# Modulation vector taken from TensorE to VectorE and ScalarE, one reciprocal for the delta net's head norms, early gates in two banks

## The reference, cut to what matters

```python
# the modulation: one vector for the tokens (c_2), one for the context (c_ctx_2);
# of silu(c) @ mod_w + mod_b the second block takes a shift, a scale and a gate,
# three vectors of 1024. Nothing of the first block goes into it.
h = rms_norm_2(x, norm_g) * (1 + scale) + shift
...
# the delta net's queries and keys, per head of 64 channels
def l2_normalize(x):
    return x * lax.rsqrt(jnp.sum(x * x, axis=-1, keepdims=True) + EPS)
...
# a branch's gate: a full 1024 x 1024 product of the same h for each branch
gate = jax.nn.sigmoid(h @ w_gate[i] + b_gate[i])
```

## Time and profile before

| what | value |
|---|---|
| median of 3 runs | 3339.85 us (3337.48 to 3342.76) |
| the profiled execution | 3348.89 us, its span 3347.2 us |
| mean granted clock of TensorE in it | 0.941 of full speed |
| TensorE busy | 3004.7 us, 90% of the span |
| VectorE, ScalarE, GpSimd busy | 1467.1, 912.6, 105.8 us |

### The profile page before, as it was taken

How to read it: one execution, slowest core, us unless ns; L and a number is a source line. 1 busy time by engine, 2 the same in 40 slices (tenths; PEclk the granted TensorE clock), 3 DMA queues, 4 the chain that set the end, 5 groups by cost and what they waited for, 6 DMA issues and landing times. The chain is left out here.

```text
span 3347.2 us, 33632 instructions
## 1 busy us (share of the span) xinstructions
PE 3004.7 (90%) x13728; PEld 2362.4 (71%) x13728; DVE 1467.1 (44%) x1540; ACT 912.6 (27%) x1132; POOL 105.8 (3%) x101
## 2 busy tenths in 40 slices
PE   6998999888998989889799999999849989998878
PEld 5887788766775767667477877777537768876656
DVE  2263555334313223583522222223455768842754
ACT  3131111223312243351321212112134632122122
POOL 0001111000000010010000000000000000000000
PEclk9978998899999989999899999999879999999989
DMA  3131000120011110551111111111131111112231
GB/s 137 50 127 54 26 22 26 35 73 29 28 64 50 66 40 20 186 189 38 69 44 43 45 51 44 44 44 44 75 113 38 44 57 57 57 38 90 87 116 63
DMA packets 60587, 211.35 MB, mean 63 GB/s; under 512 B 6288, under 2 KB 11312, under 8 KB 57776
## 3 DMA queue, kind: packets, MB, share of 16 engines
q1 hardware_dynamic: 54128, 178.16, 15.4%
q0 software_dynamic: 6336, 31.46, 2.7%
HBM read 170.79 MB, written 38.80 MB: 63 GB/s over the span
## 5 line engine op out<-in xcount | busy, mean ns | idle before, releaser
L275 PE MATMUL psum<-mixer_in,weights_parts 128*128 128x512 f32 x2112 | 505.4, 400 | 18.3 <-PEq L179 15.9
L413 PE MATMUL psum<-hidden,weights_parts 128*128 128x512 f32 x1536 | 462.7, 446 | 42.9 <-ACT early_gate L437 30.3
L275 PEld LDWEIGHTS psum<-mixer_in,weights_parts 128*128 128x128 f32 x2112 | 399.3, 189 | 117.4 <-issue 17.3
L413 PEld LDWEIGHTS psum<-hidden,weights_parts 128*128 128x128 f32 x1536 | 306.7, 209 | 136.4 <-issue 30.8
L242 DVE TENSOR_TENSOR weights_parts<-weights_raw,weights_parts 128x1024 fp32r<-128x1024 f32 (+2 forms) x195 | 211.2, 1083 | 422.3 <-ACT weights_parts L226 422.1
L275 PE MATMUL psum<-mlp_hidden,weights_parts 128*128 128x512 f32 x1536 | 364.8, 399 | 20.3 <-PEq L179 20.3
L275 PE MATMUL psum<-mlp_in,weights_parts 128*128 128x512 f32 x1536 | 361.2, 396 | 13.2 <-PEq L2326 8.4
L275 PEld LDWEIGHTS psum<-mlp_hidden,weights_parts 128*128 128x128 f32 x1536 | 291.9, 190 | 93.2 <-issue 21.9
L275 PEld LDWEIGHTS psum<-mlp_in,weights_parts 128*128 128x128 f32 x1536 | 288.7, 188 | 86.1 <-issue 15.2
L226 ACT CAST weights_parts<-weights_raw 128x1024 fp32r<-128x1024 f32 (+2 forms) x195 | 182.2, 935 | 439.0 <-PE psum L275 258.0
L275 PE MATMUL psum<-hidden,weights_parts 128*128 128x512 f32 x1200 | 284.3, 398 | 11.2 <-PEq L783 6.5
(11 more groups left out here) (439 smaller groups left out, 3387.1 us busy)
## 6 DMA issues: line engine op xcount, KB each, us to landing
weights_raw<-in_w_in SPq DMA_DIRECT2D x73, 512.0 KB, 3.3
weights_raw<-in_w_gate SPq DMA_DIRECT2D x32, 512.0 KB, 3.7
gate_scratch<-early_gate SPq DMA_DIRECT2D x64, 256.0 KB, 2.3
gate<-gate_scratch POOLq DMA_DIRECT2D x32, 512.0 KB, 4.3
weights_raw<-in_w_mlp_in SPq DMA_DIRECT2D x32, 512.0 KB, 3.3
weights_raw<-in_w_mlp_out SPq DMA_DIRECT2D x32, 512.0 KB, 3.3
mod_weights<-in_mod_w POOLq DMA_DIRECT2D x8, 1536.0 KB, 6.8
weights_raw<-in_w_out SPq DMA_DIRECT2D x24, 512.0 KB, 3.5
```

What stands on the lines that cost most here:

```text
L275: mm = nc.tensor.matmul(c.psum[:, bank + h, 0:cols], c.parts[:, s, wp, at], moving(k, xp, h), start=(n < halves), stop=(n >= halves * (3 * ...
L413: mm = nc.tensor.matmul(c.psum[:, bank, :], c.parts[:, s, wp, at], self.hidden[:, k, xp, h * HALF:(h + 1) * HALF], start=(k == 0 and n == ...
```

## The change: what it does

1. **Modulation.** The 192 narrow matmuls, the loads for them, the silu in the constants block and the block `modulate` are gone. The weights come in transposed: 24 tiles of 128x1024. In the first three `w_mlp_out` passes, GpSimd's queue loads the input vector, repeated on all partitions (`mod_row`), and the tiles, two at a time, into `squares`; VectorE multiplies a tile by the row, ScalarE copies it with a running sum into one column of `mod_sums`. Pass 0 does 16 tiles for the tokens' vector, pass 1 the same 16 for the context's, pass 2 the last 8 for the tokens'. VectorE finishes with five small operations. These passes are now written out eight units long instead of a loop of two.
2. **Head norms.** All four tiles' squares are summed into eight rows (one for each head of queries and keys) by matmuls with 8 output channels; one root and one reciprocal on 8x1024 follow; four matmuls with 8 input rows spread them to the heads' partitions, and VectorE multiplies straight from the banks. Silu of the last two tiles comes behind the squares.
3. **Loads.** Masks and row selectors of `delta_net_chunks` are loaded at the start of `delta_net_inputs`, ahead of the early gates' loads on SyncE.
4. **Banks.** Early halves use two banks in turn where both are free, and TensorE waits only for the copy of the last half that used the same bank. In the delta net these are halves 0 to 7 and from 25 on (half 24 and half 25 both get bank 7), in the other three branches halves 0 and 1 or 0 to 3, and 10 and 11.

```diff
@@ EarlyGates.pe_program
-                    if k == 0 and (half or self.h0):
-                        pe.wait_ge(self.copied, 2 * self.h0 + half)
+                    if k == 0 and self.h0 + half:
+                        same = [n for n in range(half) if self.bank(n) == bank]
+                        pe.wait_ge(self.copied, 2 * self.h0 + (same[-1] + 1 if same else 0))
@@ class Modulation
+    COLUMNS = ((0, range(2 * KT)), (1, range(2 * KT)), (0, range(2 * KT, 3 * KT)))
...
+    def load(self, pool):
+        pool.dma_start(self.row[:], self.t["mod_c"][self.column].partition_broadcast(P)).then_inc(
+            self.row_loaded, 16)
+        for m, n in enumerate(self.rows):
+            if m >= 2:
+                pool.wait_ge(self.act.sem, self.act.value(f"summed{n - 2}"))
+            pool.dma_start(self.w[:, m % 2, :], self.t["mod_w"][n]).then_inc(
+                self.loaded[m % 2], 16)
...
+    def on_act(self, a, q, j):
+        if q == 0:
+            a.wait_ge(self.row_loaded, 16 * (self.turn + 1))
+            self.nc.scalar.activation(self.row[:], self.row[:], ACT.Silu).then_inc(
+                self.act.step("silu"), 1)
+        for m, n in self.at(q):
+            a.wait_ge(self.vecs.sem, self.vecs.value(f"product{n}"))
+            w = self.w[:, m % 2, :]
+            self.nc.scalar.activation(
+                w, w, ACT.Copy, accum_out=self.sums[:, n, self.column:self.column + 1]).then_inc(
+                    self.act.step(f"summed{n}"), 1)
+
+    def on_dve(self, v, q, j):
+        if q == 0:
+            v.wait_ge(self.act.sem, self.act.value("silu"))
+        for m, n in self.at(q):
+            v.wait_ge(self.loaded[m % 2], 16 * (self.before[m % 2] + m // 2 + 1))
+            w = self.w[:, m % 2, :]
+            self.nc.vector.tensor_tensor(w, w, self.row[:], ALU.mult).then_inc(
+                self.vecs.step(f"product{n}"), 1)
@@ delta_net
-                early.begin(14, hidden, lambda half: 6 if half < 8 else 7, (t["w_in"], 10, KT))
+            early.begin(14, hidden,
+                        lambda half: 7 if 8 <= half < 25 else 6 + half % 2, (t["w_in"], 10, KT))
@@ delta_net_inputs, TensorE
-                for n, (q, j) in enumerate(((0, 0), (1, 0), (0, 1))):
-                    modulation.multiply(p, q, j)
-                    early.pe(p, g0 + 8 * n + 8)
+                early.pe(p, g0 + 32)
+                p.wait_ge(c.steps["dma"], d0 + 80)
...
+                        mm = nc.tensor.matmul(c.psum[0:8, h, :], head_sums[:, n, :],
+                                              sq[:, n, h * HALF:(h + 1) * HALF],
+                                              start=(n == 0), stop=(n == 3))
+                mm.then_inc(pes.step("sums"), 1)
+                early.pe(p, g0 + 48)
+                p.wait_ge(vecs.sem, vecs.value("rstd"))
...
+                        mm = nc.tensor.matmul(c.psum[:, spread_to[n] + h, :], head_rows[0:8, n, :],
+                                              root[0:8, h * HALF:(h + 1) * HALF],
+                                              start=True, stop=True)
@@ the other branches
-        early.begin(6, hidden, lambda half: 4, (t["w_in"], 19, KT))
+        early.begin(6, hidden, lambda half: 4 if 2 <= half < 10 else 4 + half % 2,
+                    (t["w_in"], 19, KT))
-            early.begin(6, hidden, lambda half: 7, (t["w_in"], 13, KT))
+            early.begin(6, hidden, lambda half: 7 if 4 <= half < 10 else 6 + half % 2,
+                        (t["w_in"], 13, KT))
-                early.begin(6, hidden, lambda half: 7, (t["w_gate"][:, :, D:], 0, 2))
+                early.begin(6, hidden, lambda half: 7 if 4 <= half < 10 else 6 + half % 2,
+                            (t["w_gate"][:, :, D:], 0, 2))
@@ mlp
+                how = dict(dve_per_unit=1, dve_epilogue=add if chunk else copy, banks_read_by="dve",
+                           unroll=8, background={"pool": column.load, "act": column.on_act,
+                                                 "dve": on_dve})
```

More of the change, by code:

```diff
@@ L585, in _ @@
                 nc.vector.memset(c.eps[:, n:n + 1], value).then_inc(vecs.step("eps"), 1)
-        @block.scalar
-        def _(act):
-            act.wait_ge(dma.sem, 64)
-            nc.scalar.activation(c.silu[:], vec(c, "c_2", 0, 16), ACT.Silu).then_inc(
-                silu.step("silu"), 1)
-    silu.end()
-    c.base["dma"] = 64
+    c.base["dma"] = 48
     vecs.end()
@@ new lines, in __init__, with begin @@
+    def __init__(self, nc, c, t, buffers, ctx):
+        self.nc, self.c, self.t, self.w = nc, c, t, buffers
+        self.row = c.sb("mod_row", [P, D], ctx=ctx)
+        self.sums = c.sb("mod_sums", [P, 3 * KT, 2], ctx=ctx)
+        self.row_loaded = c.sem("mod_row_loaded")
+        self.loaded = [c.sem(f"mod_weights_loaded_{s}") for s in range(2)]
+        self.turns = [0, 0]
+    def begin(self, turn):
+        c = self.c
+        self.turn = turn
+        self.column, self.rows = self.COLUMNS[turn]
+        self.act = Steps(c, "act", ["silu"] + [f"summed{n}" for n in self.rows])
+        finish = ["mod", "scale", "times", "plus", "gate"] if turn == 2 else []
+        self.vecs = Steps(c, "vec", [f"product{n}" for n in self.rows] + finish)
+        self.act.end()
+        self.vecs.end()
+        self.before = list(self.turns)
+        self.turns = [n + len(self.rows) // 2 for n in self.turns]
+        return self
@@ new lines, in load, with at @@
+    def load(self, pool):
[6 more added lines that the diff above has]
+                self.loaded[m % 2], 16)
+    def at(self, q):
+        each = len(self.rows) // KT
+        return [(m, self.rows[m]) for m in range(each * q, each * q + each)]
@@ L876, with delta_net @@
 DN_MASKS = 9
-def delta_net(nc, c, t, hidden, small, modulated, early):
+def delta_net(nc, c, t, hidden, small, early):
     with ExitStack() as ctx:
@@ L899, in delta_net, with delta_net_inputs @@
         early.end()
-def delta_net_inputs(nc, c, t, proj, rows, g_tok, small, modulation, padded_rows, early):
+def delta_net_inputs(nc, c, t, proj, rows, g_tok, small, padded_rows, masks, select, early):
     with ExitStack() as ctx:
         conv = c.sb("dn_conv_out", [P, 2, S], ctx=ctx)
-        sq = c.sb("dn_squares", [P, 2, S], ctx=ctx)
-        root = c.sb("dn_norms", [P, 2, S], ctx=ctx)
+        sq = c.sb("dn_squares", [P, 4, S], ctx=ctx)
+        root = c.sb("dn_norms", [P, S], ctx=ctx)
+        head_sums = c.sb("dn_head_sums", [P, 4, 8], ctx=ctx)
+        head_rows = c.sb("dn_head_rows", [P, 4, P], ctx=ctx)
         restart = c.sb("dn_chunk_restart", [P, S], ctx=ctx)
@@ L957, in _ @@
                                      ACT.Exp).then_inc(act.step("rate"), 1)
-                for n in range(4):
-                    a.wait_ge(pes.sem, pes.value("sums", n))
-                    if n >= 2:
-                        a.wait_ge(vecs.sem, vecs.value("unit", n - 2))
-                    nc.scalar.activation(root[:, n % 2, :], c.banks(2 * (n % 3)),
-                                         ACT.Sqrt, bias=c.eps[:, 0:1]).then_inc(act.step("root"), 1)
-                    early.act(a, g0 + 32 + 8 * n)
+                early.act(a, g0 + 48)
                 a.wait_ge(vecs.sem, vecs.value("to_end"))
@@ L1037, in _ @@
+                p.wait_ge(vecs.sem, vecs.value("rstd"))
+                for n in range(4):
                     if n == 3:
-                        modulation.multiply(p, 1, 1)
-                        early.pe(p, g0 + 32)
-                        p.wait_ge(act.sem, act.value("root", 0))
+                        p.wait_ge(vecs.sem, vecs.value("unit", 0))
                     for h in range(NH):
-                        mm = nc.tensor.matmul(c.psum[:, 2 * (n % 3) + h, :], c.head_ones[:],
-                                              sq[:, n % 2, h * HALF:(h + 1) * HALF],
+                        mm = nc.tensor.matmul(c.psum[:, spread_to[n] + h, :], head_rows[0:8, n, :],
+                                              root[0:8, h * HALF:(h + 1) * HALF],
@@ L1044, in _ @@
                                               start=True, stop=True)
-                    mm.then_inc(pes.step("sums"), 1)
-                for j in range(2, MOD_LOADS // 2):
-                    for q in range(2):
-                        early.pe(p, g0 + 32 + 16 * (j - 2) + 8 * q + 8)
-                        modulation.multiply(p, q, j)
+                    mm.then_inc(pes.step("spread"), 1)
+                early.pe(p, g0 + 56)
                 p.wait_ge(act.sem, act.value("tail"))
+                p.wait_ge(vecs.sem, vecs.value("unit", 1))
@@ L2535, in branches @@
             project(nc, c, t["w_in"], 0, 2, hidden, small, (t["w_in"], 2, KT))
-            delta_net(nc, c, t, hidden, small, modulated, early)
+            delta_net(nc, c, t, hidden, small, early)
             latent_attention(nc, c, t, hidden, small, early)
@@ L3406, in build @@
         gate = c.sb("mod_gate", [P, KT])
-        merged, x = branches(nc, c, t, x_ctx, merged_ctx, (times, plus, gate))
```

(6 more changed lines are left out.)

191 lines of the change are left out of this document (81 added, 110 removed), and 2 rows, old and new, of the table n.

## The result

| | before | after |
|---|---|---|
| median | 3338.66 us (4 runs, 3337.15 to 3342.76) | 3246.91 us (4 runs, 3245.40 to 3254.51) |
| profiled execution | 3348.89 us, span 3347.2, granted clock 0.941 | 3254.51 us, span 3252.7, granted clock 0.946 |

After to before is 0.9723, interval 0.9701 to 0.9745: 92 us less. The prediction said 74 us less, 3266 us. The measured time lies under the forecast's range (3250 to 3284), and just under the bottom of the wider one (3247). The direction and the main term held; 18 us were not in the sum.

The account below looks back on a forecast made before the run. TensorE's own work and waits were taken as the bound, with VectorE and ScalarE waiting in delta_net_inputs. Savings of 63 + 10 + 0.7 = 74 us took the median from 3339.85 to 3266 us, range 3250 to 3284 (8 in 10: 3247 to 3294).

Parts of the forecast that it names:

- Part 1: delta_net_inputs: with the narrow matmuls gone and selectors loaded earlier, 63 us saved, bounds 55 to 66.
- the walk: delta_net_inputs: step-by-step timeline through VectorE, ScalarE, VectorE and TensorE, putting the spreading of rows at 227.1 instead of 290.1.
- two gaps of about 4 us: delta_net_inputs: TensorE idle near 165 for ScalarE's copy and near 204 for VectorE's first product.
- 2.5 us of surcharge: delta_net_inputs: charged once for a half slowed by the lower clock behind TensorE's second gap.
- Part 2: Two banks for early halves: fewer copy waits, 10 us saved, bounds 4 and 13; 5.85 in the forgetting attention's inputs.
- Part 3: Kernel start: the modulation's silu and one small load leave ahead of the first load of x; 0.7 us saved.
- Part 4: MLP: the modulation's products, running sums and tile loads fit inside units of 11.4 us and cost nothing.
- the hold on GpSimd's loads that the rule weighed would have added: MLP tile loads: VectorE operations locking a port would lengthen each landing by about 2.5 us, to 6.8; sum unchanged.
- The shuffle of the chunks' steps: Delta net chunks: four of eight steps slow, may become none or all; 10 us either way, not counted.
- Cold inputs: Rival, delta_net_inputs: short fp32 products and gaps keep TensorE's clock low; 50 us saved, 3290 us; chance 0.16.
- Banks that do nothing: Rival, early halves: ScalarE's copies are only late by something else; 3276 us, inside the forecast's range.
- Loads holding up the MLP, partly or wholly: Rivals, MLP: partly, 10 us landings cost 38 us, 3304 us, chance 0.07; wholly, 12.8 us landings, 3349 us, 0.03.

Follow-up runs that it names:

- e3: The changed kernel with 640 unused bytes per partition behind the last constant, so later tiles lie at the old kernel's addresses; 3273.96 us, ratio to before 0.9790.
- e8: The kernel before with only the two alternating banks for early halves added; 3326.72 us, ratio to before 0.9954.
- e9: The changed kernel with 128 unused bytes per partition, moving tiles at distance 192 from the weights modulo 256; 3261.78 us, one run.
- e12: The changed kernel with 192 unused bytes per partition, moving tiles at distance 0 from the weights modulo 256; 3238.33 us, one run.
- e2: The changed kernel, unchanged, profiled and timed once more; 3251.88 us, ratio to before 0.9737.
- e14: The changed kernel, unchanged, timed a third time; 3247.82 us, ratio to before 0.9721.
- e13: The changed kernel with 192 unused bytes at one end of SBUF and 96 at the other, all moving tiles at distance 0; 3228.48 us, ratio 0.9660.
- e6: The kernel before with 384 unused bytes per partition behind the small constants, nothing else changed; 3324.43 us, ratio to before 0.9945.
- e15: The kernel before with 64 unused bytes per partition, nothing else changed; 3311.64 us, ratio to before 0.9906.

## Where the prediction was right, and which step failed

- **Part 1, 63 us: right in size, in part by terms that cancel.** Measured 63.6; 72.95 us for the block in e3 too, so it owes next to nothing to the spacing. Over all profiles the block takes 133.7 to 136.3 us in the kernels that have the old one and 71.7 to 73.3 in the others: 62 us less by the means. Up to the decay chain the walk held step by step: reciprocal 6.54 us (taken 6.55), VectorE's decay chain begun 46.7 us behind the block's start (walked: 200.5 - 153.8 = 46.7). Behind it, the fourth spreading took 3.77 us instead of 1.8, and the turning with the block's end about 2 us less than walked. Of the two gaps of about 4 us, the first came (3.98 us) and the second was only 0.48. The half behind it took 7.97 us all the same, about the 2.5 us of surcharge over 5.7, but not for the reason given: the clock had fallen to 0.50 during the products with 8 rows ahead of the gap. That this term fits is luck. No run separates what the modulation, the single reciprocal and the earlier loads gave; of the 63.6, the wait for the selectors is 8.1.
- **Part 2, 10 us: the main item right, the rest sized too low.** At the old spacing the three attention stages gave 2.3 + 1.1 + 9.2 = 12.6 us in e3 and 15.5 in e8. I had costed 2.1, nothing and 6.6, which is 8.7 (the other 1.4 of the ten lie in the delta net). In the forgetting attention's inputs the copy waits went altogether: from the first early half to the first scores it was 35.5 us before and is 29.6 in e3 and 29.5 in e8, 5.9 us less, where 5.85 were costed. Of the other 3.3 and 2.3 us of that stage 0.7 was costed; I have no row for the rest. The gated linear attention, costed at nothing, gave 1 to 2 us. The latent attention's stage has two lengths, by the execution: with the two banks 240 us in e8 and most others, 244 in e3, e9 and e12. That is the difference between 5.3 and 2.3.
- **Part 3, 0.7 us: right.** The first load of x is issued at 4.49 us instead of 5.29, since it no longer comes behind the silu and a small load, and TensorE starts at 18.99 instead of 19.69.
- **Part 4, nothing: right**, 0.1 us a pass by e3. L measured 3.7 us in the median (4.3 taken), so the hold on GpSimd's loads that the rule weighed would have added does not show there; for the longest landings, up to 10.2 us, no row gives a reason.
- **The shuffle of the chunks' steps: right in kind and size.** ScalarE's starts of the steps in the changed kernel:
```profile
225.53 0.41 ACT L1226 COPY dn_k<-dn_projected 128x256 f32<-128x256 f32 x1 [7.86 <-POOL dn_u L1208]
...
260.43 0.41 ACT L1226 COPY dn_k<-dn_projected 128x256 f32<-128x256 f32 x1
...
304.70 0.41 ACT L1226 COPY dn_k<-dn_projected 128x256 f32<-128x256 f32 x1
...
349.00 0.41 ACT L1226 COPY dn_k<-dn_projected 128x256 f32<-128x256 f32 x1
```
 The first step takes 34.9 us, 6.6 less than before (most of it only because ScalarE's start stood 3.6 us ahead of the spreading of rows before and stands 1.8 behind it now), and those that follow 44.3, the slow length of the earlier trace rows. In e2, the same kernel, three of them took 41.8, and the stage 386.6 us instead of 394.1; in e14 it took 379.9. Over all profiles it takes 379 to 382 us at a granted clock of 0.96 to 0.97 and 394 at 0.90. So it goes by the execution, not by the kernel; in this profile it hides 4 us of the gain.
- **The step that failed** is none of the four parts. It is a term that the sum put at nothing without a reason: that the stretches whose code is unchanged keep their time, a matmul of this shape taking the 0.237 us of the earlier trace rows before and after. Some 5,000 of them, in streams whose moving tile slid from distance 192 to 64, became 4.4 ns shorter, most of them in any one execution: 22 us by the medians of e2 and e3, 18 by their ratios. 66 us for the edits and 22 for the addresses make the 88 us of e2 (70 and 18 by the ratios). The first is what the prediction was about, and its 74 us lie inside e3's interval.
- **The rivals.** Cold inputs: no, the clock was 0.88, and the saving 63.6. Banks that do nothing: no, by e8. Loads holding up the MLP, partly or wholly: no, by the passes of e3 and the landings.

What stays open: why the distance matters (the runs show that it does, and not what in the chip makes it so), and why single streams of a kernel at distance 64, as the two `w_mlp_out` passes here, run at 233.3 ns in one execution and at 229 in another, while none at 0 and none at 192 does.

## What to carry to other kernels

Take an edit's time from the stages, not from the total: first compare, between two traces, the stages that were not edited. If they moved, something else moved with them, here the addresses. An edit that adds or drops even a small constant is then tested with unused bytes put in its place, as in e3; and where TensorE is the bound, trying a few sizes of them (e12, e13) adds no instruction and gave here 19 us more.

Narrow products that held TensorE for 58 us held two idle engines and the clock with them: with them gone, one reciprocal for four and the loads issued earlier, their stage became 62 to 64 us shorter. At their new place, which has slack of whole units, they cost 0.1 us a pass.

## What the runs showed of the hardware

- The split matmuls of 128x512 in an unbroken stream are 226.7 to 233.3 ns apart at a granted clock of 1.00, by where in SBUF the moving tile starts relative to the weights, modulo 256 bytes: best at 0, worst at 96 and 192 of the five distances tried. At 0, 96 and 192 every long stream keeps to it; at 64, 16 of 104 run at 233.3 ns. Nothing else in the kernel needs to change: e6 and e15 gain 20 and 31 us by unused bytes alone.
- A reciprocal of rows of 1024 takes the same on few partitions as on all: 6.54 us on 8, 6.55 on 128. Other lengths were not tried.
